# The memory's key and value products of a two-block transformer: moved in the last gather stage, and turns joined to the linear stages that follow

## What is computed

```
def peer(h, wq, sub_keys, u_tab, v_tab):            # 128 tokens at a time
    q = (xc @ wq).reshape(C, 8, 2, 128)
    s = einsum('chpd,hpnd->chpn', q, sub_keys)
    s1, i1 = top_k(s[:, :, 0], 16); s2, i2 = top_k(s[:, :, 1], 16)
    top, pos = top_k(s1[..., :, None] + s2[..., None, :], 16)   # eidx: 8*16 = 128 experts a token
    g = softmax(top)
    a = gelu(einsum('chkd,cd->chk', u_tab[eidx], xc))
    return einsum('chk,chkd->cd', g * a, v_tab[eidx])

def memory_cross_attention(h, mem_n, wq, wk, wv, wo):
    q = h @ wq; k = mem_n @ wk; v = mem_n @ wv      # k and v need only the given memory
    ...
second block, per layer:
    h = rms_norm(x, norm_mix_w[l]); x = x + hybrid_mixer(h, ...)
    hq = rms_norm(x, norm_xq_w[l]); mem_n = rms_norm(mem, norm_mem_w[l])
    x = x + memory_cross_attention(hq, mem_n, w_mq[l], w_mk[l], w_mv[l], w_mo[l])
```

## Time and profile before

| | us |
|---|---|
| median of 3 runs | 3897.51 (3883.25 to 3909.63) |
| the profiled execution, its own time | 3898.61 |
| its span, first to last instruction | 3896.8 |
| last gather stage, first row of U0 to last row of V1 | 2319.8 to 3114.4 |
| rows of U0, V0, U1, V1 begin | 2319.8, 2542.8, 2734.9, 2940.2 |

### The profile page before, as it was taken

The page is one execution under the profiler, slowest core; times in us unless marked ns, Lnnn a source line. Parts: engine busy times, 40 slices in busy tenths (PEclk is TensorE's granted clock), DMA queues, the critical chain, the costliest instruction groups (busy, mean ns, idle before and its releaser), DMA issues. The chain is left out here.

```text
span 3896.8 us, 31188 instructions
## 1 busy us (share of the span) xinstructions
PE 2855.6 (73%) x8573; PEld 1468.2 (38%) x8573; DVE 2519.7 (65%) x5633; ACT 798.7 (20%) x2041; POOL 1682.2 (43%) x1722
## 2 busy tenths in 40 slices
PE   8998675868787675742377864577457799999988
PEld 3455532214552232210123462222222265566555
DVE  3656978787795778878754478577866535523552
ACT  2233200212122101210123320022002202410331
POOL 2324555665456655656663346457656500000000
PEclk9989887887899887976698985689569999999999
DMA  7535699999999999989996469899999944133422
GB/s 268 187 110 173 246 397 387 337 355 327 372 346 364 339 398 407 361 304 359 365 353 235 141 234 374 325 357 363 367 380 340 344 163 146 65 133 138 146 86 81
DMA packets 353190, 1088.65 MB, mean 279 GB/s; under 512 B 32640, under 2 KB 41340, under 8 KB 351996
## 3 DMA queue, kind: packets, MB, share of 16 engines
q0 software_dynamic: 232592, 849.45, 57.9%
q1 hardware_dynamic: 120428, 237.22, 17.3%
HBM read 1081.26 MB, written 5.29 MB: 279 GB/s over the span
## 5 line engine op out<-in xcount | busy, mean ns | idle before, releaser
L2204 ACT ACTIVATE heads<-common,dots 128x128 f32<-128x128 f32 x768 | 282.7, 397 | 792.7 <-PE psum L2220 383.8
L1238 PE MATMUL psum<-ring,turned 128*128 128x512 f32 (+2 forms) x864 | 365.9, 581 | 66.7 <-issue 43.9
L2170 DVE SCALAR_TENSOR_TENSOR lent<-lent,psum 128x1024 f32<-128x1024 f32 x274 | 322.6, 1217 | 51.1 <-ACTq L475 27.9
L2220 PE MATMUL psum<-proj,heads 128*128 128x512 f32 x374 | 212.8, 672 | 181.6 <-issue 148.9
L2220 PE MATMUL psum<-lent,heads 128*128 128x512 f32 x524 | 294.1, 667 | 66.4 <-DMA lent<-in_peer_v_dram,picks_u 28.6
L2258 POOL DMA_INDIRECT lent<-in_peer_u_dram,picks_u x274 | 256.9, 938 | 188.8 <-DVE lent L2170 95.2
L1242 PE MATMUL psum<-turned,ring 128*128 128x256 f32 x640 | 207.5, 453 | 164.6 <-issue 149.1
L2258 POOL DMA_INDIRECT lent<-in_peer_v_dram,picks_u x262 | 251.8, 961 | 162.4 <-issue 57.1
L1238 PEld LDWEIGHTS psum<-ring,turned 128*128 128x128 f32 x864 | 174.9, 204 | 255.6 <-issue 233.0
L1686 PE MATMUL psum<-ring,turned 128*128 128x512 f32 x512 | 235.2, 618 | 35.1 <-DVE mixed L1736 9.6
L2178 DVE SCALAR_TENSOR_TENSOR psum<-lent,dots,psum 128x512 f32<-128x512 f32 x262 | 197.9, 755 | 86.7 <-DMA lent<-in_peer_v_dram,picks_u 58.1
(11 more groups left out here) (361 smaller groups left out, 5304.8 us busy)
## 6 DMA issues: line engine op xcount, KB each, us to landing
ring<-in_w_in_dram SPq DMA_DIRECT2D x35, 2048.0 KB
lent<-in_w_in_dram SPq DMA_DIRECT2D x11, 2048.0 KB, 7.9
proj<-in_ada_w_dram POOLq DMA_DIRECT2D x20, 1024.0 KB, 5.7
heads<-in_ada_w_dram POOLq DMA_DIRECT2D x20, 1024.0 KB, 6.0
ring<-in_w_out_dram SPq DMA_DIRECT2D x10, 2048.0 KB
ring<-in_peer_wq_dram SPq DMA_DIRECT2D x10, 2048.0 KB
lent<-in_w_out_dram SPq DMA_DIRECT2D x4, 2048.0 KB, 9.2
ring<-in_w_mk_dram SPq DMA_DIRECT2D x4, 2048.0 KB
```

The lines of the kernel that those rows point to most:

```text
L1238: mm = pe.matmul(psum[:, b % nb, 0:cols], lhs(k, it), w[:, kk, :], start=k == 0, stop=k == k_total - 1)
L2170: dve.scalar_tensor_tensor(out=src, in0=src, scalar=1.0, in1=kept_row, op0=ALU.mult, op1=ALU.mult, accum_out=weight).then_inc(rows_used.se ...
L2204: act.activation(diags[n % DIAGS], ident, ACT.Copy, scale=dots[:, j:j + 1]).then_inc(diag_ready.sem, 1)
L2220: pe.matmul(kept_row[:, 0:512], diags[n % DIAGS], row_slot(r)[:, 0:512], start=j == 0, stop=j == PICKS - 1).then_inc(pe_rows.sem, 1)
```

## The change

1. The load of the memory and of the second block's tables leaves the last gather stage's start for an attention stage before it (`first_attention(0, load_second)`).
2. The memory's mean squares and its scaling stand beside the linear stage of `w_out` (`memory_root`, `ahead`), and the transposes with layer 0's gain stand at the end of TensorE's work in the keys stage (`turn_memory`). The two normalization guests and the guest that waited for the memory are gone.
3. Layer 0's key products open the gather stage, ahead of the softmax and the gates; its value products follow those.
4. Layer 1's transposes and key products stand beside the second search in V0 (`keys_beside_search`), and only its value products are left in U1.
5. Nothing is stored to HBM inside the gather stage. Layer 1's keys stay on the chip (in `stream`), and the other three pieces (1 MB each) are stored in the second block's first linear stage, one behind each weight load (`store_memory`). What is fetched back is 2 MB for layer 0 and 1 MB for layer 1, in the linear stage of `w_mq_2` (`fetch_memory`).
6. The four raw turns are joined to the linear stages behind them (`RawTurn`): a product waits for the half of the turned columns that it reads. The matmuls of `roots_ahead` stand before the fourth group rather than the second.
7. The search of layer 1's second tile uses part of `gate_rows` as scratch; the gelu uses another row of it.

```diff
+    class RawTurn:
+        def __init__(self, gain, home, tiles=(0, 1)):
...
+            self.groups = [(half, t) for half in range(2) for t in tiles]
...
+        def await_half(self, pe, half):
+            n = len(self.tiles)
+            if half == 0:
+                pe.wait_ge(*read_v.at(n if n > 1 else 1))
+            else:
+                if n > 1:
+                    pe.wait_ge(*read_v.at(self.count - 1))
+                pe.wait_ge(*read_a.at(1))
...
-                        if ahead and len(ahead) > 2 and b == 1:
+                        if ahead and len(ahead) > 2 and b == 3:
                             ahead[2](pe)
...
+                            if turn and b == 0 and k % 4 == 0:
+                                turn.await_half(pe, k // 4)
...
-                    yield 10.3 if hosted() and g == 0 else 6.9, g + 1
+                    yield 3.5 if job[1] == "cols" else 10.3 if hosted() and g == 0 else 6.9, g + 1
...
+                for g in range(4):
+                    gain_memory_pair(act, 0, g, g)
...
-                for i, _ in enumerate(search_work(dve, t)):
-                    yield 2.6 if i % 3 == 2 else 2.2
+                for i, _ in enumerate(search_work(dve, t, l=l)):
+                    us = 2.6 if i % 3 == 2 else 2.2
+                    yield (us, i + 1) if i < marked else us
...
-        norms = [lambda l=l: memory_norm(l) for l in range(DEPTH)]
-        memory = [(lambda l=l: memory_products(l), wide, 4 * PICKS, True) for l in range(DEPTH)]
-        experts_stage(0, gate_row(0, 1), [begun[0]] + beside([lambda: probabilities(0), await_memory, lambda: expert_gates(range(1)), norms[0]], wide)
-                      + memory[:1] + [PICKS] + search(1, 1) + beside(norms[1:], wide) + memory[1:], load_second)
+        experts_stage(0, gate_row(1, 1), [begun[0], (lambda: memory_keys(0), wide, 4 * PICKS, True)]
+                      + beside([lambda: probabilities(0), lambda: expert_gates(range(1))], wide)
+                      + [(lambda: memory_values(0), wide, 4 * PICKS, True), PICKS]
+                      + beside([lambda: topk_stage(1, 1, keys_beside_search)], slim, 2 * PICKS)
+                      + [(lambda: memory_values(1), wide, 4 * PICKS, True)])
...
+    def keys_beside_search(l):
...
+        def tensor(pe):
+            yield 1
+            pe.wait_ge(*values_done)
+            for g in range(4):
+                turn_memory_pair(pe, g, g)
+            for b in range(2):
+                w = take(pe, ("w_mk_2", l, b))
+                for c in range(4):
+                    n = 4 * b + c
+                    yield 2 + n
...
+                    for k in range(KD):
+                        mm = pe.matmul(psum[:, n % 6, 0:256], w[:, k, c * P:c * P + P], turned_s[1][:, k, :],
+                                       start=k == 0, stop=k == KD - 1)
...
+    def store_memory(sp):
+        def parts():
+            for j in range(2):
+                yield sp.dma_start(memory_kv[:, j, :], (memory_k, memory_v)[j][0]).then_inc(*stored.one(16))
+            yield sp.dma_start(memory_v1, memory_v[1]).then_inc(*stored.one(16))
```

More of the change, by code:

```diff
@@ L1114, in turn_stage, with tensor @@
         run_stage(tensor, vector, scalar, sync)
-    def raw_turn_stage(gain, sync=None):
-        open_stage()
-        def tensor(pe):
-            for g in range(4):
+    class RawTurn:
+        def __init__(self, gain, home, tiles=(0, 1)):
+            self.gain, self.home, self.tiles = gain, home, tiles
+            self.groups = [(half, t) for half in range(2) for t in tiles]
+            self.count = len(self.groups)
+        def tensor(self, pe):
+            for i, (half, t) in enumerate(self.groups):
@@ L1136, in vector, with scalar @@
                 ins.then_inc(*read_v.one())
-        def scalar(act):
+            dve.wait_ge(*ready_a.at(2))
+        def scalar(self, act):
+            if len(self.tiles) > 1:
+                self.squares(act)
+            i, (half, t) = self.count - 1, self.groups[-1]
+            act.wait_ge(*products.at(i + 1))
+            for q in range(4):
+                k = 4 * half + q
+                ins = act.activation(self.home[:, k, t * P:t * P + P], psum[:, i, q * P:q * P + P], ACT.Copy, scale=self.gain(k, t))
+            ins.then_inc(*read_a.one())
+            if len(self.tiles) == 1:
+                self.squares(act)
@@ L1141, in scalar @@
                                accum_out=stats[:, t:t + 1]).then_inc(*ready_a.one())
-            act.wait_ge(*products.at(4))
-            for q in range(4):
-                ins = act.activation(turned_s[0][:, 4 + q, P:2 * P], psum[:, 3, q * P:q * P + P], ACT.Copy, scale=gain(4 + q, 1))
-            ins.then_inc(*read_a.one())
-        run_stage(tensor, vector, scalar, sync)
     roots = stats[:, 60:62]
@@ L1172, in roots_ahead, with linear_stage @@
         return vector, scalar, tensor
-    def linear_stage(jobs, beside=None, sync=None, ahead=None):
+    def linear_stage(jobs, beside=None, sync=None, ahead=None, turn=None):
         open_stage()
@@ L1205, in product @@
         def product(g):
-            return products.at(after(g) + 1)
+            return products.at((turn.count if turn else 0) + after(g) + 1)
         def tensor(pe):
             g = 0
+            if turn:
+                turn.tensor(pe)
             for job in jobs:
@@ new lines, in memory_root, with turn_memory_pair, gain_memory_pair @@
+        return vector, scalar
+    def turn_memory_pair(pe, g, bank):
+        for i in range(2):
+            k = 2 * g + i
+            for t in range(2):
+                mm = pe.transpose(psum[:, bank, 256 * i + P * t:256 * i + P * t + P], mixed_v[:, 2 + t, k * P:k * P + P], ident)
+        mm.then_inc(*filled.one())
+    def gain_memory_pair(act, l, g, bank):
+        act.wait_ge(*filled.at(g + 1))
+        for i in range(2):
+            k = 2 * g + i
+            ins = act.activation(turned_s[1][:, k, :], psum[:, bank, 256 * i:256 * i + 256], ACT.Copy,
+                                 scale=column("norm_mem_w_2", 8 * l + k))
+        ins.then_inc(*emptied.one())
@@ L2569, in small_work @@
+    def store_memory(sp):
[3 more added lines that the diff above has]
+            yield sp.dma_start(memory_v1, memory_v[1]).then_inc(*stored.one(16))
+        waiting = parts()
+        issue_loads(sp, waiting, 1)
+        for _ in waiting:
+            pass
     def small_work(l):
```

143 lines of the change are left out of this document (94 added, 49 removed).

## The result

The changed kernel takes 3840.64 us (median of 6 runs, 3834.12 to 3851.33), the kernel before 3892.66 beside it (6 runs): a ratio of 0.9861, with a 95% interval of 0.984 to 0.9882. That is 52 us, where the prediction had 38. The profiled execution took 3851.33 us, its span is 3849.5.

The account below looks back on a forecast made before the run. DMA was taken to bound the last gather stage, except where DVE waits for late products. U0 -14, V0 +10, U1 -28 and turns -6 sum to -38 from 3898.6; forecast 3860 us, 8-in-10 range 3838 to 3888.

Parts of the forecast that it names:

- the opening wait: At U0's softmax, DVE waits behind the keys' evictions from about 2360 for some 30 us, of which 12 are lost.
- what bounds the stage: Last gather stage: DMA engines bound it at 358 to 383 GB/s, except two holes where DVE waits for late products.
- the price of bytes: Last gather stage: each phase's bytes divided by its shown rate, such as 382 or 383 GB/s, give its time.
- Rival D: U phases: stops go but gathers fall to V1's 358 GB/s, so only -12 us, 3887; chance 0.06.
- U0, "a gain of 14": Gather stage's first phase: 197 us of transfers plus 12 of opening wait make 209 for 223.
- rival A: Opening of U0: the memory's keys pass fast, no wait, 12 us more gained, 3848; chance 0.25.
- Rival C: End of U0: the hole at row 120 returns smaller, DVE waits 10 to 20 us, 3875; chance 0.17.
- V0, "a loss of 10": Stage's second phase: added value blocks make 72.3 MB, 199 us at 364 GB/s, plus 3 for crowding: 202.
- rival B: V0: TensorE's starved pace comes in, +133 (+35) us, 3993 (3895), slower than before; chance 0.07.
- U1, "a gain of 28": Stage's third phase: 6.3 MB leave, 67.9 MB at 383 take 177 us; the values end before row 112.
- The turns, "6 us": Four raw turns joined to linear stages: first product some 1.5 us earlier each, 6 us, bounds 2 and 10.
- What I cost at nothing: Moved load, memory's squares and scaling, transposes and three stores fit idle places: 0 us; transposes cost 4 if cover went.

Follow-up runs that it names:

- changed_third: The changed kernel with no edit, run again later on another occasion: 3815.75 us, ratio to the kernel before 0.9835.
- keys1_in_u1: Changed kernel with layer 1's key products back in U1, in one linear stage with its values, transposes still beside the search: 3830.93 us, ratio to before 0.9893.
- stores_back: Changed kernel with an extra 2 MB store to HBM behind each layer's values inside the gather stage: 3826.33 us, ratio to before 0.9868.
- keys0_behind: Changed kernel with layer 0's keys behind the softmax and gates, in one linear stage with the values: 3851.24 us, ratio to before 0.9857.
- keys_left: Changed kernel with both layers' key products back in the U phases, everything else of the change kept: 3832.10 us, ratio to before 0.9868.
- norm1_back: Changed kernel with layer 1's key products back in U1 and its normalization heading U1 again, no transposes beside the search: 3855.18 us, ratio to before 0.9921.
- turns_apart: Changed kernel with the four raw turns as stages of their own again: 3820.41 us, ratio to before 0.9853.

## Why the prediction was right, and where it wasn't

The forecast of 3860 with a range of 3838 to 3888 holds the result, though near its lower end. The direction was right, and so were the opening wait and what bounds the stage, in part; V0, the cause in U1 and the price of bytes were not. That the sum came within 14 us owes something to luck: in the profiled pair the parts give 21 us more than forecast and a late entry takes 12 of them back, and by the medians of the two later pairs with the changed kernel the gain is 59 and 69 us, not 38. By its steps:

*What bounds the stage.* Right that it is DMA: with the holes gone the stage moves at 377 GB/s instead of 359. The whole stage before:

```profile
2320.00:3114.00 794.00, 478.73 (x942) 195.48 (x942) 558.97 (x1065) 120.69 (x328) 474.59 (x500) 0.75 0.94 359
```

and in changed_third:

```profile
2302.00:3040.00 738.00, 413.94 (x925) 174.12 (x925) 552.56 (x1038) 105.51 (x296) 472.96 (x501) 0.77 0.99 377
```

Rival D (the rate falls to 358) is out. The price that I put on bytes was wrong. I divided all bytes of a phase by the rate of 382 or 383. Two value blocks in U1 took at most 1 us where that gives 11 (keys1_in_u1), and a store of 2 MB took nothing (stores_back): rows go on at one in 1.4 us, and the other transfers come mostly on top, up to 403 GB/s over a U phase.

*U0, "a gain of 14".* Measured 20, and 25 and 24 in the two other executions. The opening wait is there, so rival A is out. Counted from U0's begin it was to stand from 40 to 70 us, and it stood from 52 to 68. The end was right, and DVE did the 38 rows that I had counted. I let them take as long as they need to land; DVE needs 1.14 us for each, 43 us in all, and spent some 9 us idle or on the softmax between them. The term that was mis-sized is its price. I took 12 us; the stretch moved 310 GB/s for 27 us where 390 stood before it, which is 5.5 us lost. With the forecast's 197 us of transfers that gives 203, the measured time, in part by luck: U0 moved 379 GB/s for 203 us, 77 MB, where I had counted 75.3. Rival C (a smaller stop at row 120) did not come in the changed kernel; it is what keys0_behind and keys_left show.

*V0, "a loss of 10".* This step failed: V0 is 3 us shorter, not 10 longer (2 and 6 shorter in the others). I used the rate of the stretch behind the search, 364, for all of V0, and a crowding term of 3. The measured -3 lies between that and the lower bound that I had written down, -7. Beside the search DMA had room, and the added work filled it. First norm1_back, which has no keys there:

```profile
2507.00:2597.00 90.00, 71.14 (x132) 24.48 (x131) 70.35 (x234) 25.05 (x69) 54.35 (x58) 0.91 0.93 348
```

and then changed_third, which has them:

```profile
2501.00:2591.00 90.00, 86.73 (x273) 49.88 (x271) 75.39 (x257) 27.60 (x85) 56.18 (x60) 0.99 1.00 382
```

These are V0's first 90 us in both. TensorE goes from 71 to 87 us of busy time, DMA from 348 to 382 GB/s, and POOL still issues two rows more (60 for 58). By bytes the gathers' queue moved 30.2 MB for 31.3, and the value blocks came with 4.1, so 3 MB of them were on top. The clock is 0.99 for 0.91. Shown is that the keys don't cost the forecast's 10 us; that they gain any isn't clear: V0 lasts 191 to 195 us in the five profiles without keys there (before is one), and 186 to 195 in nine with them. Of rival B (the starved pace in V0) nothing came, although TensorE was as full as I had worked out.

*U1, "a gain of 28".* Right in size (26, 28 and 26), wrong in the cause. I had 16 of the 28 us from bytes that leave, and keys1_in_u1 has two thirds of these bytes in U1 and lasts 178.1 us: the size came out by luck. The rest was to come from the keys leaving the U phase. Of the normalization I wrote that its "DVE work is hidden by gathers". The work is; its *place in front of the products* isn't. norm1_back against keys1_in_u1 is 25 us of U1 for that one guest, and 24 against keys_left in the same group. That the late start carries these 25, and not something else in the guest, is read from the order of the records and wasn't isolated. The reasoning missed that a `parted` guest starts ahead of the phase when nothing stands before it. The trace of before had it: the first key product 9.5 us after U1's begin, with waits for DVE and for the meeting ahead of it.

*The turns, "6 us".* Right for what it counted, too small for the whole. Against before the first product comes 2.2 us earlier at the first turn and 1.3 at each other, 6.0 together. The tail gives 9.2, and turns_apart's 10.5. Between the first product and the sixtieth record behind it another 4 us go, at the first three turns; I put nothing there, and what they are isn't shown.

*What I cost at nothing.* The load, the root and the transposes stand ahead of the stage. From TensorE's record 4061 to its record 4851 in the keys stage, which spans the load and the root, it is 199.9 us before and 0.5 to 1.3 more in the three executions of the changed kernel. From record 4851 to U0's begin, with the transposes on the way, it is 19.7 us before and 19.4 to 19.6 in the three. The three stores show no cost in the tail: turns_apart has them, and its tail is before's.

By the profiled pair: -20 - 3 - 26 - 1 - 9 = -59 for the forecast's -38, and +12 of a later entry give the -47 between the two profiles. For the parts, with what was taken out: both keys' places 10 us of stage time (keys_left against changed_third, 16 by medians), layer 1's normalization ahead of U1 25, the turns 4 to 10. U0 with its keys behind the gates is still 18 us below before (205.0 for 223.0). By the pattern of U1 that would be layer 0's normalization and its meeting; the guest that waited for the memory's load left U0 as well. No run put either back, so it is argued, not shown. Nor do I know that these parts would add up in another order.

## What to carry to other kernels

When work is late, look at what stands between it and its earliest start, not only at how fast it runs. A small guest that makes engines meet cost 25 us in U1; taking it away did more than moving the products to another phase. Don't price a transfer by its bytes at the rate of the gathers before trying it: two blocks of 2 MB cost U1 at most 1 us, and beside the search, where the DMA share was 0.93, two blocks took the place of 1 MB of rows. And a marker in one engine's order delays only that engine.

## What the runs showed of the hardware that I had not expected

- In the U phases of this stage TensorE falls to one matmul record in 1.2 to 1.8 us after some 48 to 70 quick ones (116 where it started ahead of the phase), while DMA is full with gathers. The pace is per matmul, or per weight load, and not per column (128 columns: 1.59 us, 256: 1.17 to 1.76, the last from 17 records in 30 us in changed_third). It is absent beside little loaded DMA (127 records in 30 us) and returns within a few microseconds when gathers run dry (160 in 20 us). Full DMA alone doesn't make it: in V0 of changed_third 92 records pass in 30 us at 407 GB/s. The granted clock of 0.50 in such stretches goes with it, but the gaps of up to 2.4 us between matmuls of 0.38 us are "issue", not slow matmuls.
- The Trainium skill, Runtime: NRT & Kernel Launch, section "Instruction fetch mechanics", says that the sequencer fetches its instructions through a DMA queue of its own, ahead of need, and that the cost is mostly hidden. A fetch that has to share with saturated gathers would fit the quick start. The trace rather speaks against it. The profile records packets of instruction queues, and of 36 us within the slow stretch of changed_third (2322 to 2358) it shows none; all packets are the gathers', while some 20 matmul records pass:

```profile
q0 software_dynamic: 3714, 13.52, 99.6%
```

  The quick pace is back at 2357.2, ahead of the next such packet at 2362.9. No run changed the fetching, and the cause of the slow pace stays open.
- A store of 2 MB beside such gathers cost them nothing (410 and 415 GB/s in the stretches with a store, 25 rows in 35 us). Loads of weights cost hardly more: U1 with 4.2 MB of them more had 126 rows in 177 us at 403 GB/s, and 127 in 176 at 388 without them.
- With TensorE's 128 extra key records and 16 transposes in V0 the granted clock beside the search was 0.99 for 0.91, and V0 was no longer for them.
